# Seven-product steps 1, 2, 4 and 5 in every panel, products combined and gated on GpSimd, and a ring of six in the feed-forward

## The reference

```python
def hybrid_layer(x, mem, ...):
    u = rms_norm(x, norm_g) @ w_in
    ...                                   # four branches: sparse attention, retention, hgrn2, memory
    for n, (y, z) in enumerate(...):
        merged = merged + sigmoid(gate_all[:, :, n]) * ((y * silu(z)) @ w_branch[n])
    return x + merged @ w_out

def hybrid_layer_2(x, ...):
    ...
    gt, up = split(rms_norm_2(x, g_ffn) @ w_gate_up, 2, axis=-1)
    return x + (silu(gt) * up) @ w_down   # 2 x 5632 columns up, 5632 rows down
```

## Time and profile before

| what | value |
|---|---|
| median of 3 runs | 3272.59 us (3271.31 to 3272.82) |
| the profiled execution | 3272.8 us, of which the span from first to last instruction is 3271.0 us |
| granted TensorE clock, mean | 1.000 |
| TensorE matmul (PE) busy | 3258.1 us, 15091 matmuls |
| VectorE (DVE) busy | 2203.4 us |
| ScalarE (ACT) busy | 1638.9 us |
| GpSimd (POOL) busy | 321.3 us |
| moved by DMA | 619.77 MB |

### The profile page before, as it was taken

How to read it: one execution, slowest core, us unless ns; L and a number is a source line. 1 busy time by engine, 2 the same in 40 slices (tenths; PEclk the granted TensorE clock), 3 DMA queues, 4 the chain that set the end, 5 groups by cost and what they waited for, 6 DMA issues and landing times.

```text
span 3271.0 us, 39924 instructions
## 1 busy us (share of the span) xinstructions
PE 3258.1 (100%) x15091; PEld 2699.7 (83%) x15091; DVE 2203.4 (67%) x2476; ACT 1638.9 (50%) x2085; POOL 321.3 (10%) x282
## 2 busy tenths in 40 slices
PE   8999999999999999999999999999999999999999
PEld 7888888888888888888888888888888888888887
DVE  5466655588865656555888655575555578888887
ACT  6444445455544444454555445455444455555554
POOL 0111241100000102411000011160000100000000
PEclk9999999999999999999999999999999999999999
DMA  8665565666666655556665675554565656556655
GB/s 300 191 185 166 165 177 162 188 206 193 217 193 205 182 167 166 173 164 186 202 211 183 208 226 170 172 179 144 193 192 183 186 187 204 187 194 204 194 193 180
DMA packets 303808, 619.77 MB, mean 189 GB/s; under 512 B 24961, under 2 KB 29441, under 8 KB 302465
## 3 DMA queue, kind: packets, MB, share of 16 engines
q1 hardware_dynamic: 303616, 617.22, 60.9%
HBM read 609.80 MB, written 7.34 MB: 189 GB/s over the span
## 4 chain that ended last, share of the span: by engine, by line
PE 100%; DMA 0%; DVE 0%; ACT 0%; SPq 0%; issue 0%
PE G L1127 69%; PE X L1048 6%; PE X L1046 6%; PE X L1047 6%; PE X L826 2%; PE G L1048 2%; PE G L1047 2%; PE G L1046 2%; PE X L942 1%; PE X L914 1%; PE G L1121 1%; PE X L969 0%; PE X L968 0%; PE X L935 0%; PE X L916 0%; PE X L889 0%
## 5 line engine op out<-in xcount | busy, mean ns | idle before, releaser
L1452 DVE TENSOR_TENSOR w_lo<-raw,w_hi 128x1024 fp32r<-128x1024 f32 (+1 forms) x1016 | 1236.9, 1223 | 942.2 <-ACT w_hi L1148 915.4
L1148 ACT ACTIVATE w_hi<-raw 128x1024 fp32r<-128x1024 f32 (+1 forms) x1016 | 1052.8, 1041 | 1265.3 <-PE G L1127 1129.0
L1127 PE MATMUL G<-w_hi,xh 128*128 128x512 f32 x1984 | 796.0, 401 | 0.0
L1127 PE MATMUL G<-w_hi,xl 128*128 128x512 f32 x1984 | 775.0, 391 | 0.0
L1127 PE MATMUL G<-w_lo,xh 128*128 128x512 f32 x1984 | 772.7, 389 | 0.0
L1127 PE MATMUL G<-w_hi,yh 128*128 128x512 f32 x1256 | 499.3, 398 | 8.5 <-DVE w_lo L1452 8.5
L1127 PE MATMUL G<-w_hi,yl 128*128 128x512 f32 x1256 | 491.2, 391 | 0.0
L1127 PE MATMUL G<-w_lo,yh 128*128 128x512 f32 x1256 | 490.0, 390 | 0.0
L1127 PEld LDWEIGHTS G<-w_hi,xl 128*128 128x128 f32 x1984 | 372.3, 188 | 81.0
L1127 PEld LDWEIGHTS G<-w_hi,xh 128*128 128x128 f32 x1984 | 372.9, 188 | 73.9 <-issue 2.7
L1127 PEld LDWEIGHTS G<-w_lo,xh 128*128 128x128 f32 x1984 | 373.3, 188 | 72.2
(11 more groups left out here) (261 smaller groups left out, 3164.3 us busy)
## 6 DMA issues: line engine op xcount, KB each, us to landing
raw<-in_w_in SPq DMA_DIRECT2D x572, 512.0 KB, 3.6
raw<-in_w_gate_up SPq DMA_DIRECT2D x176, 512.0 KB, 4.1
raw<-in_w_down SPq DMA_DIRECT2D x88, 512.0 KB, 4.5
raw<-in_w_out SPq DMA_DIRECT2D x64, 512.0 KB, 4.2
raw_more<-in_w_in SPq DMA_DIRECT2D x52, 512.0 KB, 4.4
raw<-in_w_branch SPq DMA_DIRECT2D x48, 512.0 KB, 3.8
raw<-in_w_mem_kv SPq DMA_DIRECT2D x32, 512.0 KB, 6.3
raw<-in_w_o SPq DMA_DIRECT2D x32, 512.0 KB, 3.6
```

The costliest lines, as they stand in the source:

```text
L1127: mm = M.matmul(G[blk.g][:, t, :], a[:, blk.kk + k, tok], ringed(w, blk, c)[:, j, :], start=(k == 0 and q == 0), stop=(k == blk.kt - 1 and ...
L1148: A(high_of(c)[:, 0:size_of(c)], source_of(c), ACT.Copy).then_inc(hi_done, 1)
L1452: V.tensor_tensor(low_of(c)[:, 0:n], source_of(c), high_of(c)[:, 0:n].bitcast(F32), ALU.subtract).then_inc(lo_done, 1)
```

## The change

- `SEVEN` is (1, 2, 4, 5): four steps of each panel in the seven-product form in place of three, now in two adjacent pairs. There are four forms to make for each group of panels instead of three (`forms` index 3, `x_forms` index 3).
- In the feed-forward the two extra slots are used too: `Block.wide` now holds for FF panels and for `down` of j of 1 and more. `EXT_FIRST` and `EXT_LOAD` have an entry for `FF`, with waits for the tensors under the extra slots.
- `cross` moves from VectorE to GpSimd, its four additions unchanged; GpSimd takes it as soon as `stem` has signalled both `G`.
- `silu_product` moves to GpSimd, as two products of 128x1024 in place of four operations of 128x512. GpSimd's product takes no scale, so `wide_sigmoid` for FF panels gets two more ScalarE operations of 128x1024, which scale `sig_wide` in place after a wait on ScalarE's own semaphore `gate_read`; `wide_sig` is signalled after them.

```diff
@@ -32,7 +32,7 @@
 STEPS = KD // 2
-SEVEN = (1, 3, 5)
+SEVEN = (1, 2, 4, 5)
@@ -133,7 +133,7 @@
         at += b.chunks
-        b.wide = (b.kind == "panel" and b.name[1] != FF) or (b.name[0] == "merge" and b.name[1] < DEPTH and ("panel", *b.name[1:3], b.name[3] // 2) in panels)
+        b.wide = b.kind == "panel" or (b.name[0] == "down" and b.name[1] > 0) or (b.name[0] == "merge" and b.name[1] < DEPTH and ("panel", *b.name[1:3], b.name[3] // 2) in panels)
@@ -210,8 +210,8 @@
 BEHIND = {c: range(max(R_BEHIND[c], 0), R_BEHIND[c + 1]) for c in range(N_CHUNKS)}
-EXT_FIRST = {l: [min(c for c in range(FIRST_WIDE[l], N_CHUNKS) if U_SLOT[c] == k) for k in (4, 5)] for l in range(DEPTH)}
-EXT_LOAD = {l: min(r for r, (b, _s) in enumerate(LOADS) if b >= FIRST_PANEL[l] and R_SLOT[r] >= RING) for l in range(DEPTH)}
+EXT_FIRST = {l: [min(c for c in range(FIRST_WIDE[l], N_CHUNKS) if U_SLOT[c] == k) for k in (4, 5)] for l in PANEL_EVENTS}
+EXT_LOAD = {l: min(r for r, (b, _s) in enumerate(LOADS) if b >= FIRST_PANEL[l] and R_SLOT[r] >= RING) for l in PANEL_EVENTS}
@@ -1141,10 +1141,14 @@
                     act.wait_ge(mm_done, U_PREV[c] + 1)
-                for l in range(DEPTH):
+                for l in PANEL_EVENTS:
...
-                        act.wait_ge(y_ready, Y_OF["norm", "b", l, H - 1] + 1)
-                        act.wait_ge(o_squared, NORM_OF["norm", "b", l, H - 1] + 1)
+                        if l == FF:
+                            act.wait_ge(y_ready, Y_OF["s_pv", "l", 2, HEADS2 - 1] + 1)
+                            act.wait_ge(x_sq_done, 16)
+                        else:
+                            act.wait_ge(y_ready, Y_OF["norm", "b", l, H - 1] + 1)
+                            act.wait_ge(o_squared, NORM_OF["norm", "b", l, H - 1] + 1)
@@ -1168,6 +1172,10 @@
                         last = A(hidden[:, t, :], sig_wide[:, t, 0:NB], ACT.Sigmoid, scale=by[:, t:t + 1])
+                    last.then_inc(gate_read, 1)
+                    act.wait_ge(gate_read, FF_PANEL[b] + 1)
+                    for t in range(TT):
+                        last = A(sig_wide[:, t, :], sig_wide[:, t, :], ACT.Copy, scale=by[:, t:t + 1])
@@ -1451,14 +1459,6 @@
 
-            def cross(b):
-                freed(dve, b)
-                link(V.tensor_tensor(six, sig_wide[:, 0, 0:NB], six, ALU.add))
-                V.tensor_tensor(sig_wide[:, 0, NB:], six, five, ALU.add)
-                link(V.tensor_tensor(sig_wide[:, 1, 0:NB], six, sig_wide[:, 1, 0:NB], ALU.add))
-                V.tensor_tensor(sig_wide[:, 1, NB:], sig_wide[:, 1, 0:NB], five, ALU.add).then_inc(crossed, 1)
@@ -1467,18 +1467,6 @@
                     V.tensor_tensor(sig_wide[:, t, :], both, sig_wide[:, t, :], ALU.add).then_inc(x_banks_free, 1)
-            def silu_product(b):
-                dve.wait_ge(wide_sig, PANEL_N[b] + 1)
-                for t in range(TT):
-                    last = V.scalar_tensor_tensor(out=hidden[:, t, :], in0=sig_wide[:, t, 0:NB], scalar=x_rs[FF][:, t:t + 1], in1=hidden[:, t, :],
-                                                  op0=ALU.mult, op1=ALU.mult)
-                link(last)
-                for t in range(TT):
-                    last = V.scalar_tensor_tensor(out=hidden[:, t, :], in0=sig_wide[:, t, NB:], scalar=x_rs[FF][:, t:t + 1], in1=hidden[:, t, :],
-                                                  op0=ALU.mult, op1=ALU.mult)
-                last.then_inc(hidden_ready, 1)
@@ -1780,10 +1768,6 @@
                         read_out(ENDS[e])
-                    if e - 2 in STEM_ENDS:
-                        cross(STEM_ENDS[e - 2])
-                    if e - 2 in ENDS and ENDS[e - 2] in FF_PANEL:
-                        silu_product(ENDS[e - 2])
@@ -1863,6 +1847,20 @@
                 V.tensor_tensor(f[:, 3, :], a12, f[:, 1, :], ALU.subtract).then_inc(forms_ready, 1)
+            def cross(b):
+                freed(pool, b)
+                link(V.tensor_tensor(six, sig_wide[:, 0, 0:NB], six, ALU.add))
+                V.tensor_tensor(sig_wide[:, 0, NB:], six, five, ALU.add)
+                link(V.tensor_tensor(sig_wide[:, 1, 0:NB], six, sig_wide[:, 1, 0:NB], ALU.add))
+                V.tensor_tensor(sig_wide[:, 1, NB:], sig_wide[:, 1, 0:NB], five, ALU.add).then_inc(crossed, 1)
+            def silu_product(b):
+                pool.wait_ge(wide_sig, PANEL_N[b] + 1)
+                link(V.tensor_tensor(hidden, sig_wide[:, :, 0:NB], hidden, ALU.mult))
+                V.tensor_tensor(hidden, sig_wide[:, :, NB:], hidden, ALU.mult).then_inc(hidden_ready, 1)
@@ -1908,6 +1906,9 @@
                     output_norm()
+                for b in PANELS:
+                    if BLOCKS[b].name[1] == l:
+                        cross(b)
@@ -1947,6 +1948,9 @@
                 x_forms(FF, i)
+            for b in FF_PANEL:
+                cross(b)
+                silu_product(b)
```

More of the change, by code:

```diff
@@ L587, in hybrid_program @@
         sums_done, forms_ready, forms_done, form_rounded = sem("sums_done"), sem("forms_ready"), sem("forms_done"), sem("form_rounded")
-        crossed, x_banks_free, wide_sig, hidden_ready = sem("crossed"), sem("x_banks_free"), sem("wide_sig"), sem("hidden_ready")
+        crossed, x_banks_free, wide_sig, gate_read, hidden_ready = sem("crossed"), sem("x_banks_free"), sem("wide_sig"), sem("gate_read"), sem("hidden_ready")
         hi_done, lo_done, mm_done = sem("hi_done"), sem("lo_done"), sem("mm_done")
```

## The result

| | before | after |
|---|---|---|
| median | 3272.28 us (3271.31 to 3272.82) | 3301.44 us (3300.01 to 3304.1) |
| the profiled execution, its span | 3272.8, 3271.0 us | 3300.69, 3298.9 us |
| granted TensorE clock, mean | 1.000 | 0.996 |

The ratio is 1.009, 95% interval 1.0073 to 1.0108: 29 us slower, where 7 were forecast and 15 was the end of the range.

What follows compares the result with a forecast made beforehand. TensorE alone was taken to bound the kernel, so only removed matmuls or added waits count: -12.9 + 0.2 + 18.3 + 1.3 = +6.9 us, forecast 3279.5 us (+0.21%), range 3269 to 3287.

Steps and rivals of the forecast that it cites:

- Direction and place: After each feed-forward panel, TensorE starts chunk E + 4 2.03 us late behind the first `down` block's addition: nine times, 18.3 us.
- GpSimd's product: In the feed-forward, GpSimd's first product takes 1.90 us and VectorE's split of E + 7 ends 1.07 us after it.
- Products far from 1.90 us: Sign in the trace after feed-forward panels: GpSimd's products far from 1.90 us would show the prediction wrong.
- Matmuls: One more seven-product step saves 3 matmuls in each of 19 panels: 57 x 0.2267 = 12.9 us off TensorE.
- VectorE's lead in the layers: In the layers' panels VectorE stays ahead, lowest 0.1 us in each layer's first panel; cost 0.2 us, bounds 0 and 1.5.
- the fourth form: Before the first feed-forward panel, making this form delays TensorE once by 1.3 us, bounds 0.9 and 1.5; nothing in the layers.
- The later waits are covered then: In the feed-forward, GpSimd's second product and the last `h_feed` piece come before TensorE needs them: no further wait.
- Cover holds: Rival: TensorE does not meet the late read-out behind feed-forward panels and the removed matmuls stay a gain; 3261.2 us, chance 0.12.
- no lock: Rival: the split of E + 7 runs beside GpSimd's product, TensorE 1.2 us late; 3272.0 us, chance 0.15.
- Leads in the layers run out too: Rival: additions on GpSimd leave VectorE short, up to 0.5 us in 8 panels on top; 3283 us, chance 0.09.
- GpSimd keeps the lock: Rival: GpSimd holds the shared port for both feed-forward products, 4.0 us a panel; 3297 us, chance 0.07.

## Why the prediction was right or wrong

- **Direction and place: right.** The loss was put at the read-out of the first `down` block behind split E + 7, by ScalarE's queue and then GpSimd's port, and that is where it is: nine waits for L1501. Less the shift of 2.93 us, scaling ends at 2844.00 (forecast 2844.07), the product starts at 2844.08 (2844.15), and the split ends 1.09 us behind the product (1.07).
- **GpSimd's product: mis-sized.** 1.90 us was taken from L1821; it takes 2.44. L1821 reads one tensor, the product two; its own rate was in another row, 1.38 us for 128x512 with two inputs, twice that 2.76. The term came out at 21.7 us for 18.3, within its bounds. The part of it that is the port's was put at 0.83 us and is 1.40; the queue's was put at 1.2 and is 0.95, so one error hid some of the other. Products far from 1.90 us were one of the prediction's own signs of being wrong. The Trainium skill, page "GPSIMD Engine Reference", section "4.1 Engine selection", puts a two-input elementwise operation on GpSimd at about twice VectorE's time: the trace agrees, 2.44 against 1.22 us for 128x1024.
- **The clock: the step that was missing.** The sum priced a pause of TensorE at its length. A pause of 2.3 us cost another 1.57 us in seven of nine panels, 11 us, because the chunk behind it ran in part at 1.2 GHz. The runs with matmuls in the pause and with a pause made by VectorE show it from both sides. None of the rivals had it. It is the largest part of the miss, 11.0 of some 21 us, but not the whole of it: with matmuls in the pause and the clock at 1.00 the kernel still takes 3288.8 us, where the range ended at 3287. The rest is 4.2 us of matmul gain that did not come, 3.4 of the wait before E + 4 and 2.6 at the layers' ends. The Trainium skill, page "TensorE: Matmul & The Clock Gate", section "Wait — 56ns, not 53.3ns?", gives 426.7 ns from start to start for 512 columns at the low clock: the trace agrees (2853.05 to 2853.48).
- **Matmuls: count right, gain put too high.** 57 went, at 0.2267 us a piece 12.9 us, but only 8.7 were gained. The prediction held that no row speaks against it and that the extra slots could only keep the gain. They cost 0.36 us a feed-forward cycle by themselves, 9 x 0.36 = 3.2 of the 4.2 us that are missing: an edit costed at nothing.
- **The layers' ends: missed.** The change of the ring's phase by two more chunks a panel was not followed to the place where the ring narrows. 2.6 us, mended by moving `gather`. The prediction had TensorE waiting nowhere but behind the feed-forward panels and before the first of them.
- **VectorE's lead in the layers: right** (no wait in any of ten panels), and so was **the fourth form** (1.3 us forecast, 1.4 found, gone when made earlier).
- **"The later waits are covered then": right only under the long wait.** `h_feed`'s last low part was put 1.1 us ahead of the next panel. It is not late in the changed kernel, but with a shorter pause TensorE waits 0.55 us for it, and 0.9 us with the addition moved.
- **Rivals.** *Cover holds* (3261) fell, *no lock* fell (the split did take 2.62 us). *Leads in the layers run out too* fell as well. *GpSimd keeps the lock* came near the measured time with 3297, and by luck: the addition, with one input in PSUM, ran in 1.21 us right beside the second product.

What stays open: why five of 18 like pauses left the clock alone (not by their length: these are 2.12 to 2.21 us long, the other thirteen 2.11 to 2.22), and why chunks in the extra slots run about 1% longer. No run asked for either.

## What to carry to other kernels

A pause of the engine that bounds the kernel is not always worth its own length: read the granted clock in the stretch behind it, and ask for each new wait of 2 us or so what the work after it will run at. Before work goes to another engine, follow what is queued behind every instruction that the move adds, here two copies in front of one split in front of one addition, and price the loss against the slack of the whole chain: two delays of 2.2 and 1.4 us against 1.2 of slack cost 0.95 and 0.2 alone and 2.3 together. When a change alters the number of chunks, walk the ring to the places where it widens and narrows.

## What the hardware showed that was not expected

- TensorE's clock fell behind idle times that the trace records as 2.1 to 2.2 us in 13 of 18 cases (two kernels), and behind none of nine of 1.4 to 1.5 us and nine of 0.7 to 0.8, nor behind one of 1.9 (the first layer's end in the kernel with nine matmuls). The fall comes with the restart or up to 1.5 us after it; in the pause itself the granted clock is 1.00.
- Idle matmuls in a pause cost nothing and gave back 12.7 us; three of them (0.7 us) did as well as nine.
- Twelve matmuls take 2.75 to 2.77 us in the slots laid over other tensors and in slot 0 behind them, 2.72 elsewhere.
